# TensorE's order in the decode stage: units taken singly, and units taken in twos

## The reference, cut to what matters

```python
def fox_sample(q, k_new, v_new, logf_new, k_past, v_past, logf_past):
    k_all = jnp.concatenate([k_past.astype(k_new.dtype), k_new], axis=1)
    v_all = jnp.concatenate([v_past.astype(v_new.dtype), v_new], axis=1)
    ...
    c = jnp.cumsum(lf_all, axis=1).transpose(0, 2, 1)
    s = jnp.einsum('bqhd,bkhd->bhqk', q, k_all, preferred_element_type=F32) * FOX_SCALE
    s = s + cq[..., :, None] - c[:, :, None, :]
    ...
    p = jax.nn.softmax(s, axis=-1).astype(v_all.dtype)
    return jnp.einsum('bhqk,bkhd->bqhd', p, v_all)
```

## Time and profile before

| what | value |
|---|---|
| median of 3 runs | 2446.04 us (2444.86 to 2446.36) |
| span of the profiled execution | 2443.4 us |
| median less that span | 2.6 us |
| TensorE busy over the span | 2247.8 us (92%) |
| decode stage in the profile | about 929.5 to 1383 us |

### The profile page before, as it was taken

One profiled execution on the slowest core, in us unless ns is written; L12 is line 12 of the kernel. 1 busy time (PEld: TensorE's weight loads), 2 busy tenths in 40 slices (PEclk: granted clock), 3 DMA queues, 4 the chain that ended last, 5 costly groups with the idle time before them and its releaser, 6 DMA issues. The chain is left out here.

```text
span 2443.4 us, 30994 instructions
## 1 busy us (share of the span) xinstructions
PE 2247.8 (92%) x11248; PEld 1816.3 (74%) x11248; DVE 967.1 (40%) x1501; ACT 924.4 (38%) x1456; POOL 643.8 (26%) x386
## 2 busy tenths in 40 slices
PE   6999999899999788999999699699999999995999
PEld 5999999777777566666666378477778888773687
DVE  3334444453853856777776610310023211111000
ACT  4233332223443334777776510422233333334100
POOL 1222112220220000456555641111231111123420
PEclk8999999999999889999999899699999999997999
DMA  6122223202201215999998552522233222215431
GB/s 157 30 54 54 49 49 79 69 9 62 62 1 44 60 40 189 314 316 318 318 309 300 181 157 88 183 74 73 73 111 108 72 72 72 72 38 161 143 99 54
DMA packets 257337, 287.93 MB, mean 118 GB/s; under 512 B 69498, under 2 KB 168700, under 8 KB 257084
## 3 DMA queue, kind: packets, MB, share of 16 engines
q1 hardware_dynamic: 240474, 252.78, 33.2%
q10 hardware_dynamic: 16738, 33.53, 3.7%
HBM read 246.03 MB, written 41.26 MB: 118 GB/s over the span
## 5 line engine op out<-in xcount | busy, mean ns | idle before, releaser
L226 PE MATMUL bank<-whi,x_hi 128*128 128x512 f32 (+1 forms) x1536 | 592.5, 386 | 21.3 <-POOL wlo L206 16.1
L228 PE MATMUL bank<-wlo,x_hi 128*128 128x512 f32 (+1 forms) x1536 | 579.4, 377 | 0.0
L230 PE MATMUL bank<-whi,x_lo 128*128 128x512 f32 (+1 forms) x1536 | 579.0, 377 | 0.0
L226 PEld LDWEIGHTS bank<-whi,x_hi 128*128 128x128 f32 x1536 | 292.9, 191 | 83.7 <-POOL wlo L206 20.6
L259 ACT ACTIVATE projected<-bank 128x512 f32<-128x512 f32 (+1 forms) x160 | 92.2, 576 | 620.2 <-PE bank L230 590.9
L230 PEld LDWEIGHTS bank<-whi,x_lo 128*128 128x128 f32 x1536 | 292.5, 190 | 42.0
L228 PEld LDWEIGHTS bank<-wlo,x_hi 128*128 128x128 f32 x1536 | 293.4, 191 | 39.3 <-issue 0.7
L2358 POOL TENSOR_TENSOR dec_v_lo<-dec_v,dec_v_hi 128x1024 fp32r<-128x1024 f32 x92 | 230.1, 2523 | 220.7 <-ACT dec_v_hi L2712 220.6
L206 POOL TENSOR_TENSOR wlo<-wraw,whi 128x512 fp32r<-128x512 f32 (+1 forms) x192 | 230.5, 1233 | 32.0 <-ACT whi L199 31.9
L2527 DVE TENSOR_TENSOR dec_kt_lo<-bank,dec_kt_hi 128x512 fp32r<-128x512 f32 x256 | 170.6, 684 | 100.5 <-ACT dec_kt_hi L2702 100.0
L2702 ACT ACTIVATE dec_kt_hi<-bank 128x512 fp32r<-128x512 f32 x256 | 150.5, 596 | 106.9 <-PE bank L2386 95.7
(11 more groups left out here) (358 smaller groups left out, 3460.4 us busy)
## 6 DMA issues: line engine op xcount, KB each, us to landing
dec_k<-cache_k SPq DMA_DIRECT2D x256, 256.0 KB, 3.9
dec_v<-cache_v SPq DMA_DIRECT2D x256, 256.0 KB, 4.2
wraw<-w_in_even SPq DMA_DIRECT2D x32, 512.0 KB, 6.7
wraw<-w_in_odd SPq DMA_DIRECT2D x16, 1024.0 KB, 8.9
gv<-projected ACTq DMA_DIRECT2D x4, 2304.0 KB, 8.0
gm_v<-gv SPq DMA_DIRECT2D x8, 1152.0 KB, 6.0
m<-gm_mt ACTq DMA_DIRECT2D x8, 1056.0 KB, 4.1
wraw<-w_in_odd SPq DMA_DIRECT2D x4, 2048.0 KB, 8.4
```

The lines of the kernel that those rows point to most:

```text
L226: pe.matmul(bank[:, 0:width], e.xhi[:, k, c:c + P], e.whi[:, k, 0:width], start=(k == 0), stop=False)
L228: pe.matmul(bank[:, 0:width], e.xhi[:, k, c:c + P], e.wlo[:, k, 0:width], start=False, stop=False)
L230: mm = pe.matmul(bank[:, 0:width], e.xlo[:, k, c:c + P], e.whi[:, k, 0:width], start=False, stop=(k == KD - 1))
```

## The change

TensorE's loop takes two units at a time: the turns of both, then the scores of both, then what else the two units hold (new scores, the turns of probabilities, values), in unit order. The loops of the other engines, and what each of TensorE's steps waits for, stay as they are.

```diff
-                for u in range(UNITS * (DB - 1) + HEADS_AT):
-                    n, j = u // SLOTS, u % SLOTS
-                    if n < DB * GROUPS:
-                        turn_keys(n // GROUPS, n % GROUPS, j)
-                    if 0 < n <= DB * GROUPS:
-                        scores((n - 1) // GROUPS, (n - 1) % GROUPS, j)
-                    if rounds_at(u, NEW_AT) is not None:
-                        new_scores(rounds_at(u, NEW_AT))
-                    if rounds_at(u, TURN) is not None:
-                        turn_probabilities(rounds_at(u, TURN))
-                    if rounds_at(u, TURN + 1) is not None:
-                        turn_new(rounds_at(u, TURN + 1))
-                    for r, p in pieces_at(u, 0):
-                        values(r, p)
+                for first_unit in range(0, UNITS * (DB - 1) + HEADS_AT, 2):
+                    n, at = first_unit // SLOTS, first_unit % SLOTS
+                    for j in (at, at + 1):
+                        if n < DB * GROUPS:
+                            turn_keys(n // GROUPS, n % GROUPS, j)
+                    for j in (at, at + 1):
+                        if 0 < n <= DB * GROUPS:
+                            scores((n - 1) // GROUPS, (n - 1) % GROUPS, j)
+                    for u in (first_unit, first_unit + 1):
+                        if rounds_at(u, NEW_AT) is not None:
+                            new_scores(rounds_at(u, NEW_AT))
+                        if rounds_at(u, TURN) is not None:
+                            turn_probabilities(rounds_at(u, TURN))
+                        if rounds_at(u, TURN + 1) is not None:
+                            turn_new(rounds_at(u, TURN + 1))
+                        for r, p in pieces_at(u, 0):
+                            values(r, p)
```

## The result

| | before | after |
|---|---|---|
| median | 2446.20 us (4 runs on the same chip) | 2428.16 us (2427.01 to 2431.11, 4 runs) |
| ratio | | 0.9927, 95% interval 0.9912 to 0.9942 |
| span of the profiled execution | 2443.4 us | 2426.0 us |

The change is faster by 18 us. In the changed kernel, lines behind TensorE's loop stand three further down (the split on VectorE is L2530, the exponentials L2725).

What follows compares the result with a forecast made beforehand. The prediction took TensorE's work plus waits on the chain from unit 35's scores through the heads as the bound. 6.4 us at six seams and 2.1 in the last round gave 8.5 us off: 2437.5 us, range 2431 to 2445.

Steps and rivals of the forecast that it cites:

- What bounds the stage: TensorE's own work plus few waits; one chain from unit 35's scores through the heads sets ACT, DVE and TensorE free.
- Unit 35's scores earlier: At each seam, these scores and unit 41's turn come 2.1 us earlier, the new tokens' turn later on 1.48 us.
- The clock: At six seams, saving 10.8 - 1.44 f us; shorter idle makes falls rarer, giving 6.4 us, ends 10.8 and 2.2.
- f: Number of the six rounds whose seam sees the clock fall in the changed kernel, taken as 3.
- Rival B: The switch between turns and scores is cheap to save: another 8.6 us less, 2429 us; chance 0.05.
- Round 0: No heads and no values stand ahead of unit 35 there, so nothing moves earlier: 0.
- The last round: Round 7: unit 35's scores come ahead of the last values, 2.1 us saved, or 0 if value transfers lag.
- Longer runs of turns: A run of 8 turns is no cheaper than two of 4: 0, other end 8.6 us less.
- Elsewhere: Odd units' turns come up to 1.4 us earlier without new waits: 0, other end 11 us over 8 rounds.
- A: Rival: the clock falls at each seam (f = 6), 4.3 us saved, 2441.7 us; chance 0.17.
- D: Rival: transfers bind, TensorE's saved time comes back as waits for keys or values, 2446 us; chance 0.08.
- C: Rival: unit 35's scores are made but not taken earlier, 3.3 us idle, clock falls: 9.8 us slower, 2456; chance 0.11.

Runs made afterwards that it cites:

- twos everywhere but at the seam: Changed kernel with units 34 and 35 of each round taken singly, as before, all others in twos: 2455.17 us.
- turns together only: Changed kernel, but with only the turns of two units together; scores and the rest stay unit by unit: 2449.43 us.
- the pair alone: Kernel before, with units taken in twos only at units 34 and 35 of each round, all others singly: 2426.50 us.
- values behind both: Changed kernel, but each unit's turn stands just ahead of its own scores, and what else the two units hold follows behind both: 2429.37 us.
- late heads: Kernel before, with DVE computing the heads two units later and ACT storing them five units later: 2462.03 us.
- twos, copy and sums behind the piece of values: Changed kernel with the new tokens' turn one unit later on TensorE, and their copy and sums two units later on DVE: 2438.44 us.
- twos, late turn: Changed kernel with the new tokens' turn one unit later, on TensorE and for its copy and sums on DVE: 2451.62 us.

## Why the prediction was half right

**What bounds the stage: right for rounds 1 to 6.** The chain from unit 35's scores through the heads held both engines; moving those scores alone gives the whole gain, and all the rest of the change without that move gives a loss. That TensorE has no gap elsewhere was wrong (round 0, below).

**Unit 35's scores earlier: right, a little small.** The lower half is copied 2.24 us earlier and unit 41's turn comes 2.21 us earlier against unit 34's; I had 2.1 for both. ACT's wait for the heads went. The new tokens' turn comes 1.67 us earlier at full clock (13.27 and 13.30 to 11.62); I had 1.48. Together 1.1 us over the six rounds; 0.3 us of it goes again because the four falls of before had cost 1.6 us in all there, not the 1.9 of my sum.

**The clock: the step that failed.** I read falls in four of six rounds at 2.43 us of idle, took 1.8 us as the new stretch, let the falls thin out with it and took f = 3. The stretch became 1.45 us and f became 0: 4.3 us of the 7.7 us by which the stage's sum was short. The price of a fall was near: 1.44 us in my sum, and 1.6 us by the stretch of round 0 with values, which takes 41.44 us behind a fall where later rounds take 39.86 without one. Two things were wrong in it. The 1.8 us are a mixed measure: the trace counts idle time from the modelled end of a turn (1131.53 + 0.60), and I had counted from the end of its 0.43 us, which makes the new stretch 1.62 us, and had set that beside the trace's 2.43. And falls do not thin out with the length as I let them: the last table has none of 70 up to 1.46 us and four of four at 1.78 to 1.81 us, so by these counts the 1.8 us that I had would have kept the falls. Length alone does not order the counts either, for at 2.43 us four of six fell; what else decides stays open.

The clock is the largest term, but not the whole error: with f = 0 my own span ends at 2433 us, and 2428.16 came. The rest is round 0 (1.9 us), the six seams at full clock (11.5 us for 10.8), the stretches with values (0.6), what lies outside the stage (1.2), and the time around the span, which is 2.2 us in the change where I took 2.6. Rival B's 2429 us lies close to the measured time by luck: its cause, runs of eight turns, gives nothing by itself (2449.43 us), and the gain comes without them (2429.37).

**Round 0: taken as nothing, worth 1.9 us.** It is true that no score moves earlier there. But the kernel before waits 1.81 us at round 0's new tokens' turn and the clock falls behind it. The view of the earlier trace rows has that wait in a second row, with those of rounds 3 and 6, which I passed over:

```profile
PE bank L2432 <- DVE dec_pt L2582: 3.7, 3, 1.8
```

```profile
986.26 0.20 PE L2432 MATMUL bank<-ident,dec_sc_new 32*32 32x32 f32 x1 [1.81 <-DVE dec_pt L2582]
```

In the change this is 0.35 us at a turn of keys and 1.32 at the new tokens', and the clock stays; the stretch behind takes 39.73 us for 41.44.

```profile
981.15 0.66 PE L2386 MATMUL bank<-ident,dec_k 128*128 128x128 f32 x4 [0.35 <-DVE dec_kt_lo L2530]
985.19 0.20 PE L2432 MATMUL bank<-ident,dec_sc_new 32*32 32x32 f32 x1 [1.32 <-DVE dec_pt L2585]
```

It goes with the turns of two units standing together: the two other kernels that have them and keep the rest of round 0's order (twos everywhere but at the seam, turns together only) show 0.34 and 1.30, 0.33 and 1.11 us, and no fall; the four that take turn and scores unit by unit (before, the pair alone, values behind both, late heads) show 1.78 to 1.81 us and fall. The trace shows how: the new tokens' turn hardly moves (56.46 us behind the start of the stage, 56.69 before), but unit 43's turn now stands ahead of the turn of the probabilities and waits there, for the split of unit 39, so that part of the wait is spent earlier.

**The last round: right.** 2.16 us for the forecast 2.1; the transfers of values kept pace.

**Longer runs of turns: right.** A pair of units takes 1.80 us from the first turn to the first value (1123.81 to 1125.61), before 0.90 to 0.91 us for each. The mean of the first matmul of scores fell from 470 ns to this:

```profile
L2386 PE MATMUL bank<-ident,dec_k 128*128 128x128 f32 x1024 | 137.8, 277 | 17.7 <-DVE dec_kt_lo L2530 13.9 <-DMA dec_k<-cache_k 2.0 <-issue 1.8
L2404 PE MATMUL bank<-dec_kt_hi,dec_qz 128*128 128x512 f32 x256 | 107.0, 418 | 0.0
```

TensorE's busy time in the stage fell by 9 us with it (410.36 to 401.14), and almost none of that is time: durations of neighbours overlap (the row of 1125.38 lasts 0.39 us, the next one starts at 1125.61), and only starts tell. Rival B would have been read off that column.

**Elsewhere: right.** No new wait at odd units in the part with values, and none for a transfer at a DMA share of 0.89: the 2.0 us for keys in the row above stand at 952.35, early in round 0, where the kernel before waits 2.25. A and D did not come; C's time is what comes without the pair at 34 and 35.

## What to carry to other kernels

Where in-order engines wait for one another at a seam, look for the one step whose result starts the chain and put it ahead of everything that no one is waiting for; reordering the rest without it made this kernel no faster (2449 and 2455 us for 2445). Read the list of waits to its last row, and the first round by itself: a part taken as nothing was worth 1.9 us here. When the idle time before a clock fall shrinks, work the sum out with and without the falls and give both a chance, instead of a number of falls in between. Before moving an elementwise step on DVE, look at what GpSimd is doing at the new place: the cheapest step of a list can become its longest.

## What the runs showed of the hardware

**Idle time and the granted clock.** Counted over the seams of rounds 0 to 6 of all traces here, by the longest idle stretch of TensorE at the place; the rows of 2.11 and of 2.39 to 2.52 us are the waits behind the seams:

| idle ahead of a turn | where | clock fell |
|---|---|---|
| up to 1.46 us | all seven seams of the change, of its two shifted copies and of the five kernels with the late turn; rounds 1 to 6 of the pair alone and of values behind both; round 0 of twos but at the seam and of turns together only | 0 of 70 |
| 1.78 to 1.81 us | round 0: before, the pair alone, values behind both, late heads | 4 of 4 |
| 2.11 us | twos, copy and sums behind the piece of values | 3 of 3 |
| 2.43 us | before, rounds 1 to 6 | 4 of 6 |
| 2.39 to 2.52 us | twos, late turn | 7 of 7 |
| 3.08 us | rounds 1 to 6 of twos but at the seam and of turns together only | 11 of 12 |
| 4.43 us | late heads, rounds 1 to 6 | 6 of 6 |

There is no case between 1.46 and 1.78 us, and these are counts at the places of this kernel, in one profiled execution of each version.

The Trainium skill, "TensorE: Matmul & The Clock Gate", Part 4: PE-mode transpose, says that the full clock does not engage for transposes. By that rule the seams of the change would have lost it; the trace does not agree: turns stand on both sides of the wait at unit 41, with a run of eight behind it, and the clock stayed at 1.00. The longest run of turns in the stage is in the copy with 20 extra ones, 28 in a row for 3.22 us, and the clock (third column from the end) stayed at 1.00 there and behind it. A longer one was not tried.

```profile
992.75 3.22 PE L2386 MATMUL bank<-ident,dec_k 128*128 128x128 f32 x28
```

```profile
992.00:997.00 5.00, 5.00 (x38) 4.38 (x37) 2.13 (x4) 2.13 (x4) 4.22 (x2) 1.00 0.92 294
997.00:1007.00 10.00, 10.00 (x64) 7.43 (x63) 6.67 (x12) 7.34 (x12) 7.40 (x3) 1.00 0.81 278
```

**DVE beside GpSimd.** Four of DVE's steps, which read SBUF alone, lasted until GpSimd's piece had ended when they started beside one: 0.21 us became 1.91 (L2614), 0.24 became 2.25 (L2617), 0.29 became 2.49 (the queries), 1.21 became 2.88 (the values). A fifth, the rounding of the queries ahead of that step, takes about 2.3 us in the kernels before and after already, and 0.22 us with twos and the late turn. The splits, which read a PSUM bank, kept 0.67 to 0.69 us beside such pieces. The reductions and the reciprocal of the sums kept their time too, 0.13 to 0.15 us each from 1155.03 on in the kernel with twos and the late turn, though they read SBUF. The Trainium skill, "SBUF — State Buffer", section "SBUF: two separate sides", says that the two engines share one pair of ports as an exclusive lock, held for the whole instruction by whichever starts first, and that DVE needs it for two inputs in SBUF or in its two-port modes; the trace agrees, by the ends at 1147.90 and 1150.19 beside 1147.83 and 1150.14, and by the piece that starts 0.12 us ahead of GpSimd's and takes 1.21 us.
